# Maxima two tiles ahead, Fourier inputs ahead of the merge, and Fourier stages split by even and odd frequency

## The reference, cut to what matters

```python
def attend(q, k, v, lam):
    s = jnp.einsum('bhmqd,bhmkd->bhmqk', q, k, preferred_element_type=jnp.float32) * (B_QK ** -0.5)
    p = jax.nn.softmax(s, axis=-1)
    w = p[:, :, 0] - lam * p[:, :, 1]
    return jnp.einsum('bhqk,bhkv->bhqv', w.astype(v.dtype), v)

def fourier_mix(u):
    bsz, n, _ = u.shape
    uf = u.astype(jnp.float32).reshape(bsz, n, C_GROUPS, C_GROUP_DIM)
    y = jnp.fft.fft2(uf, axes=(1, 3), norm="ortho").real
    return y.reshape(bsz, n, C_WIDTH).astype(u.dtype)

def merge(y_a, y_b, y_c, mg, w_a_out, w_b_out, w_c_out, w_out):
    g_a, g_b, g_c = jnp.split(jax.nn.sigmoid(mg), N_BRANCH, axis=-1)
    y = g_a * (y_a @ w_a_out) + g_b * (y_b @ w_b_out) + g_c * (y_c @ w_c_out)
    return y @ w_out
```

## Time and profile before

| | us |
|---|---|
| median of 3 runs (2482.53 to 2489.82) | 2483.38 |
| profiled execution | 2483.57 |
| its span | 2481.80 |
| PE busy | 2329.3 (94%) |
| DVE busy | 1174.7 (47%) |
| ACT busy | 1126.4 (45%) |
| POOL busy | 726.2 (29%) |
| attention loop to the eighth z unit, layer 0 / 1 | 139.27 / 80.92 |
| from the end of cu to the first cz unit, layer 0 / 1 | 36.21 / 18.30 |

### The profile page before, as it was taken

One profiled execution on the slowest core, in us unless ns is written; L12 is line 12 of the kernel. 1 busy time (PEld: TensorE's weight loads), 2 busy tenths in 40 slices (PEclk: granted clock), 3 DMA queues, 4 the chain that ended last, 5 costly groups with the idle time before them and its releaser, 6 DMA issues.

```text
span 2481.8 us, 42435 instructions
## 1 busy us (share of the span) xinstructions
PE 2329.3 (94%) x15420; PEld 2027.9 (82%) x15420; DVE 1174.7 (47%) x2165; ACT 1126.4 (45%) x2329; POOL 726.2 (29%) x563
## 2 busy tenths in 40 slices
PE   6989999988999899999998889999989999988998
PEld 4758899858899798878886678988769989876998
DVE  3664334665335634441344663154473554436453
ACT  3454454454445534432455652222343554646443
POOL 2403554413455221122221012212222224211433
PEclk8989999989999999999999999999999999999999
DMA  7656965755865221122221012212223234221533
GB/s 286 237 183 198 313 199 186 251 195 189 289 233 199 92 83 60 56 72 98 80 78 51 26 52 97 82 52 93 87 75 102 94 106 158 70 84 52 170 136 136
DMA packets 159788, 328.73 MB, mean 132 GB/s; under 512 B 17696, under 2 KB 21024, under 8 KB 159520
## 3 DMA queue, kind: packets, MB, share of 16 engines
q1 hardware_dynamic: 159504, 325.80, 38.5%
q0 software_dynamic: 144, 0.98, 0.1%
HBM read 325.67 MB, written 1.05 MB: 132 GB/s over the span
## 4 chain that ended last, share of the span: by engine, by line
PE 77%; DVE 8%; issue 7%; ACT 4%; DMA 2%; POOL 1%; SPq 0%; POOLq 0%; ACTq 0%; DVEq 0%
PE PS L1690 15%; PE PS L1691 14%; PE PS L1692 14%; PE PS L1735 4%; PE PS L1737 4%; PE PS L1736 4%; PE PS L1671 2%; PE PS L1754 2%; PE PS L1753 2%; PE PS L1752 2%; DMA RAW<-stream 1%; PE PS L529 1%; ACT WORK L1014 1%; POOL WL L1607 1%; PE PS L1704 1%
## 5 line engine op out<-in xcount | busy, mean ns | idle before, releaser
L1607 POOL TENSOR_TENSOR WL<-RAW,WH 128x512 fp32r<-128x512 f32 x468 | 650.0, 1390 | 1680.6 <-ACT WH L1985 1680.1
L1690 PE MATMUL PS<-AR,WH 128*128 128x256 f32 (+1 forms) x2624 | 860.2, 328 | 15.0 <-DVE AR L1478 7.7
L1691 PE MATMUL PS<-AR,WH 128*128 128x256 f32 (+1 forms) x2624 | 841.6, 321 | 0.0
L1692 PE MATMUL PS<-AR,WL 128*128 128x256 f32 (+1 forms) x2624 | 841.5, 321 | 0.0
L1985 ACT ACTIVATE WH<-RAW 128x512 fp32r<-128x512 f32 x936 | 550.3, 626 | 438.9 <-DMA RAW<-stream 201.3
L2234 DVE TENSOR_TENSOR WL<-RAW,WH 128x512 fp32r<-128x512 f32 x468 | 395.9, 846 | 645.0 <-ACT WH L1985 643.3
L1690 PEld LDWEIGHTS PS<-AR,WH 128*128 128x128 f32 x2624 | 501.5, 191 | 97.9 <-issue 44.5
L1691 PEld LDWEIGHTS PS<-AR,WH 128*128 128x128 f32 x2624 | 501.8, 191 | 37.2 <-issue 2.4
L1692 PEld LDWEIGHTS PS<-AR,WL 128*128 128x128 f32 x2624 | 501.2, 191 | 36.7
L1735 PE MATMUL PS<-WH,AR 128*128 128x256 f32 x768 | 219.9, 286 | 0.0
L1736 PE MATMUL PS<-WL,AR 128*128 128x256 f32 x768 | 217.3, 283 | 0.0
(11 more groups left out here) (298 smaller groups left out, 3101.4 us busy)
## 6 DMA issues: line engine op xcount, KB each, us to landing
RAW<-stream SPq DMA_DIRECT2D x936, 256.0 KB, 2.9
WORK<-mods SPq DMA_DIRECT2D x144, 512.0 KB, 6.4
C<-consts SPq DMA_DIRECT2D x1, 1088.0 KB, 15.0
XX<-xT SPq DMA_DIRECT2D x1, 1024.0 KB, 10.2
XX<-ctxT SPq DMA_DIRECT2D x1, 1024.0 KB, 5.8
outT<-XX SPq DMA_DIRECT2D x1, 1024.0 KB, 4.8
C<-consts POOLq DMA_DIRECT2D x1, 960.0 KB, 7.5
WORK<-lam SPq DMA_DIRECT2D x1, 256.0 KB, 6.6
```

The costliest lines, as they stand in the source:

```text
L1607: pool.tensor_tensor(WL[:, u % 4, cut, :], RAW[:, (2 * u + 1) % 4, :, :], WH[:, u % 4, cut, :].bitcast(f32), ALU.subtract).then_inc(lo_don ...
L1690: pe.matmul(out, WH[:, u % 4, k, :], moving[:, 0, k, :], start=(k == 0), stop=False)
L1691: pe.matmul(out, WH[:, u % 4, k, :], moving[:, 1, k, :], start=False, stop=False)
L1692: last = pe.matmul(out, WL[:, u % 4, k, :], moving[:, 0, k, :], start=False, stop=(k == KC - 1))
```

## The change

1. `top(f+2)` follows `combine(f)` on DVE, with `top(0)` and `top(1)` ahead of the loop; `z_unit` and its weight low come one tile earlier. All eight bz units lie in the loop: a whole one ahead of it, the others from tile 1 + (x - 1) * last // 7, in three parts (9, 9 and 6 matmuls) in layer 0 and whole in layer 1.
2. The cu units stand ahead of bmerge. PE runs the four cu pairs right after the last value; heads 0 to 3 are turned after the second pair, 4 to 7 after the third. cu is no longer copied to V2: ACT copies half of each bank to FOLD and DVE writes the sum and the difference of the two token halves (`folded`). All of bmerge comes afterwards, as one loop.
3. Sums give the even frequencies, differences the odd ones, so stage one is four matmuls of 128 columns over one block for a pair of feature blocks y (an item) instead of eight. Columns of cu and cz and rows of the branch's output weights are laid out so that even and odd features of a group stand in two blocks; stage two works on them in the same way, with four matmuls an item. Items rotate over banks 4 to 7. ACT copies one half out (256 columns; in stage two the sines of both blocks) and DVE adds and subtracts; in stage two the results are interleaved, every other element. All of stage one comes ahead of stage two.

The diff, cut ("..."); of the old Fourier loops on PE, ACT and DVE only the first lines are repeated here.

```diff
-      ("bq", 8), ("bk", 8), ("bv", 8), ("bz", 8), ("bmerge", 16),
-      ("cu", 8), ("cz", 8), ("cmerge", 16), ("out", 8)]
+      ("bq", 8), ("bk", 8), ("bv", 8), ("bz", 8), ("cu", 8), ("bmerge", 16),
+      ("cz", 8), ("cmerge", 16), ("out", 8)]
...
+def unit_cuts(l):
+    return [(0, KC)] if l else [(0, 3), (3, 6), (6, KC)]
 def pieces(f, l):
-    per = per_head(l)
-    spread = [(p - 2) * (8 * per - 2) // (7 * per - 2) if p >= 2 else -1 for p in range(7 * per)]
-    return [p for p, at in enumerate(spread) if at == f]
+    parts, last = unit_cuts(l), 8 * per_head(l) - 1
+    if f < 0:
+        return [(0, p) for p in range(len(parts))]
+    begun = {1 + (x - 1) * last // 7: x for x in range(1, 8)}
+    return [(begun[f - p], p) for p in range(len(parts)) if f - p in begun]
 def ended(f, l):
-    per = per_head(l)
-    return [p // per for p in pieces(f, l) if p % per == per - 1]
+    return [x for x, p in pieces(f, l) if p == len(unit_cuts(l)) - 1]
+def fourier_items(l):
+    return [(p, y) for p in parts(l) for y in range(4)], 8 * l, 8 + 16 * l
...
-def turned_to(h, l):
-    b = stages(l)["bmerge"]
-    return (4, 6, 7, (b + 3) % 4, 5, (b + 2) % 4, 4, 6)[h]
+def turned_to(h):
+    return (4, 6, 7, 5)[h % 4]
...
-        def piece(g):
-            x, part = divmod(g, per)
-            u, ks = st["bz"] + x, KC // per
+        def piece(x, part):
+            u, (begin, end) = st["bz"] + x, unit_cuts(l)[part]
-            for k in range(part * ks, (part + 1) * ks):
+            for k in range(begin, end):
-            if part == per - 1:
+            if end == KC:
...
-            if h == 4:
+            if h == 3:
                 evicted(pe, st["bz"] + 7)
-            if h >= 6:
-                pe.wait_ge(gated, 24 * l + 8 + h - 5 + BEGUN)
+            if h >= 4:
...
+        for x, part in pieces(-1, l):
+            piece(x, part)
         for f in range(len(steps)):
             if f + 2 < len(steps):
                 score(f + 2)
             turn(f)
-            for p in pieces(f, l):
-                piece(p)
+            for x, part in pieces(f, l):
+                piece(x, part)
             if f:
                 value(f - 1)
         value(len(steps) - 1)
-        for g in range(7 * per, 8 * per):
-            piece(g)
-        for h in range(4):
-            head_turn(h)
+        for x in range(4):
+            token_pair(st["cu"], 0, 2 * x, H2, 2 * l, 4)
+            if x in (1, 2):
+                for h in range(4 * x - 4, 4 * x):
+                    head_turn(h)
         merge("bmerge", 1)
-        tokens("cu", 2 * l)
         for j in range(4):
-            pe.wait_ge(bank_read[(st["cz"] + j) % 4], earlier(st["cz"] + j))
...
+            pe.wait_ge(bank_read[(st["bmerge"] + j) % 4], earlier(st["bmerge"] + j))
+        dft = const("dft", 6 * P)
+        items, past, copied = fourier_items(l)
+        for i, (p, y) in enumerate(items):
+            if i >= 4:
+                pe.wait_ge(f1_read, past + i - 3)
+            for o in range(2):
+                x, bank = 2 * y + o, PS[:, 4 + i % 4, o * T:(o + 1) * T]
+                for e in range(2):
+                    last = pe.matmul(bank[:, e * P:(e + 1) * P], V2[:, 2 * p + e, x * P:(x + 1) * P],
+                                     dft[:, e * P:(e + 1) * P], start=True, stop=True)
+            last.then_inc(f1, 1)
+        for i, (p, y) in enumerate(items):
+            if i < 4:
+                pe.wait_ge(f1_read, past + len(items) - 4 + i + 1)
+            else:
+                pe.wait_ge(f2_read, past + i - 3)
+            for o in range(2):
+                x, bank = 2 * y + o, PS[:, 4 + i % 4, o * T:(o + 1) * T]
+                for e, (a, b) in enumerate(((0, P + 1), (P + 1, T))):
...
+        def halves(b):
+            def body(j):
+                done(b, 0, j)
+                bank = (b + j) % 4
+                if l == 0:
+                    act.activation(FOLD[:, j % 4, :], PS[:, bank, T:2 * T], ACT.Copy).then_inc(f_copied, 1)
+                elif j % 2:
+                    act.activation(FOLD[:, j % 4, :], PS[:, bank, 0:T], ACT.Copy).then_inc(bank_read[bank], 1)
+                next_high(b, 0, j)
...
+        exps(1)
         for x in ended(-1, l):
             z_unit(x)
             next_high(st["bz"], 0, x)
-        exps(1)
         for f in range(len(steps)):
             act.wait_ge(t2, tb + f + 1)
...
-        gate_functions()
-        z_unit(7)
-        next_high(st["bz"], 0, 7)
         sigmoids()
-        for k in range(KC):
-            act.wait_ge(gated, 24 * l + 8 + k + 1 + BEGUN)
-            act.activation(Y2[:, 0, k, t0:], YB[:, k, t0:], ACT.Copy).then_inc(yhi, 1)
+        take = halves(st["cu"])
+        for x in range(4):
+            take(2 * x)
+            take(2 * x + 1)
+            if x in (1, 2):
+                for k in range(4 * x - 4, 4 * x):
+                    act.wait_ge(gated, 24 * l + 8 + k + 1 + BEGUN)
+                    act.activation(Y2[:, 0, k, t0:], YB[:, k, t0:], ACT.Copy).then_inc(yhi, 1)
         merge("bmerge", 1)
-        looped(act, st["cu"], 8, 4, values(st["cu"], 2 * l))
...
+        items, past, copied = fourier_items(l)
+        for i in range(len(items)):
+            act.wait_ge(f1, past + i + 1)
+            act.activation(FOLD[:, i % 4, :], PS[:, 4 + i % 4, T:2 * T], ACT.Copy).then_inc(f_copied, 1)
+        for i in range(len(items)):
+            act.wait_ge(f2, past + i + 1)
+            if i >= 4:
+                act.wait_ge(f2_read, past + i - 3)
+            sines = PS[:, 4 + i % 4, :].rearrange("p (o t) -> p o t", o=2)[:, :, P + 1:T]
+            act.activation(SINES[:, i % 4, :, 1:P], sines, ACT.Copy).then_inc(f_copied, 1)
         z_gate("cz", 2)
...
+        def folded(j):
+            b = st["cu"]
+            if l == 0 or j % 2:
+                x = j if l == 0 else j - 1
+                row, cut = (j % 2 * 2 if l == 0 else 2), slice(j // 2 * 2 * P, (j // 2 + 1) * 2 * P)
+                if l:
+                    dve.wait_ge(bank_read[(b + j) % 4], earlier(b + j) + 1)
+                else:
+                    dve.wait_ge(f_copied, j + 1)
+                dve.tensor_tensor(V2[:, row, cut], PS[:, (b + x) % 4, 0:T], FOLD[:, j % 4, :], ALU.add)
+                ins = dve.tensor_tensor(V2[:, row + 1, cut], PS[:, (b + x) % 4, 0:T], FOLD[:, j % 4, :],
+                                        ALU.subtract)
+                ins.then_inc(bank_read[(b + x) % 4], 1)
+            next_low(b, 0, j)
...
         top(0)
+        top(1)
         for f in range(len(steps)):
-            if f:
-                combine(f)
-            for x in ended(f - 2, l):
+            combine(f)
+            if f + 2 < len(steps):
+                top(f + 2)
+            for x in ended(f - 1, l):
                 z_unit(x)
-            if f + 1 < len(steps):
-                top(f + 1)
-            if f == 0:
-                combine(0)
-            for x in ended(f - 2, l):
...
         refine(OC[:, 2, :, 2 * l:], OC[:, 3, :, 2 * l:])
-        for h in range(4):
+        for h in range(8):
             scale_head(h)
-        z_unit(7)
-        next_low(st["bz"], 0, 7)
-        for h in range(4, 8):
-            scale_head(h)
+            if h % 4 == 3:
+                folded(h // 2 - 1)
+                folded(h // 2)
         def b_low(k):
...
                               ALU.subtract).then_inc(y_done, 1)
         dve.wait_ge(bank_read[(st["bz"] + 7) % 4], earlier(st["bz"] + 7) + 1)
-        for k in range(KC):
-            dve.wait_ge(ot2, 8 * l + k + 1)
-            dve.scalar_tensor_tensor(YB[:, k, t0:], PS[:, turned_to(k, l), t0:], LM[:, 6 + l:7 + l],
-                                     SZ2[:, k, t0:], ALU.mult, ALU.mult).then_inc(gated, 1)
-            if k >= 2:
-                b_low(k - 2)
-        b_low(KC - 2)
-        b_low(KC - 1)
+        for x in range(2):
+            for k in range(4 * x, 4 * x + 4):
+                dve.wait_ge(ot2, 8 * l + k + 1)
+                dve.scalar_tensor_tensor(YB[:, k, t0:], PS[:, turned_to(k), t0:], LM[:, 6 + l:7 + l],
+                                         SZ2[:, k, t0:], ALU.mult, ALU.mult).then_inc(gated, 1)
+                if k >= 4 * x + 2:
+                    b_low(k - 2)
+            b_low(4 * x + 2)
+            b_low(4 * x + 3)
+            folded(4 + 2 * x)
+            folded(5 + 2 * x)
         merge("bmerge", 1)
-        lows("cu")
-        for p in parts(l):
...
-        dve.wait_ge(f2_read, 16 + 8 * l)
+        items, past, copied = fourier_items(l)
+        for i, (p, y) in enumerate(items):
+            dve.wait_ge(f_copied, copied + i + 1)
+            first, second = (x.rearrange("p (e c b) -> p c e b", e=2, c=2)
+                             for x in (PS[:, 4 + i % 4, 0:T], FOLD[:, i % 4, :]))
+            for o, op in enumerate((ALU.add, ALU.subtract)):
+                out = KB[:, 2 * y + o, p * T:(p + 1) * T].rearrange("p (c e b) -> p c e b", c=2, e=2)
+                ins = dve.tensor_tensor(out, first, second, op)
```

(16 more changed lines are left out.)

98 lines of the change are left out of this document (31 added, 67 removed).

## The result

The changed kernel takes 2446.11 us (median of 4 runs, 2436.42 to 2454.24) against 2486.58 of the kernel before (median of 4 in the same comparison): a ratio of 0.984, 95% interval 0.982 to 0.986. It is faster by 40 us. The forecast was 2428.7 with a range of 2412 to 2442: the sign was right, the gain of 54.9 us 14 too large, and the time 4 us outside the range. The profiled execution took 2447.45 us (span 2445.7).

What follows compares the result with a forecast made beforehand. TensorE bounds the kernel nearly everywhere, except the attention loops, bound by a circle of waits through DVE's maxima, exponentials and combine. Gains of 13.3, 3.4, 6.7, 20.7 and 10.8 sum to 54.9 us: 2483.6 to 2428.7 us, range 2412 to 2442.

Steps and rivals of the forecast that it cites:

- Part 1, layer 0: Layer 0's attention loop: maxima two tiles ahead break the circle of waits, 139.3 to 126 us, a gain of 13.3.
- The stalls: Layer 0's attention loop: TensorE waits for DVE at tiles where DVE is the later one, 16.9 us in all.
- Part 1, layer 1: Layer 1's attention loop: maxima two tiles ahead and whole z units, 80.9 to 77.5 us, a gain of 3.4.
- Part 2: cu ahead of the merge: waits of 2.7 us in layer 0 and 4.0 in layer 1 go, 6.7 us.
- The cover: cu and merge: TensorE's other work hides every later wait, tight in layer 1; otherwise 1 to 3 us return.
- Part 3: Fourier: half the matmuls and no copy wait, 15.5 and 7.5 us, gains of 20.7 and 10.8.
- disputed term: Fourier stage two on DVE, writes skipping every other element: 0.95 to 1.8 us an item, near end taken.
- A: Rival: the attention loops stay a chain of engines taking turns, +8.4 us, 2437; chance 0.14.
- B: Rival: TensorE sets nearly every loop step and half or more of the stalls goes, -15 us, 2414; chance 0.13.
- C: Rival: Fourier bound on DVE by doubled writes and slow first stage, +5 us, 2434; inside the forecast's 0.68.
- E: Rival: cover for cu and merge fails in layer 1, weights late, +3 to 6 us, 2434; inside the forecast's 0.68.
- D: Rival: waits keep TensorE's clock at its lower level throughout the loops, slower, up to 2560 us; chance 0.03.

Runs made afterwards that it cites:

- filled waits: Changed kernel with eight extra, unused matmuls ahead of each of five turns (tiles 1, 18, 22, 27, 31) in layer 0: 2432.11 us.
- Without GpSimd's overlap: Changed kernel with GpSimd's half of the weight low in layer 0 started one combine later: 2435.39 us.
- second trace: The changed kernel run and traced once more, with no edit: 2444.14 us, ratio 0.983.
- second better version: Changed kernel: z units begun per head, tile 2's score and weight low moved, last layer-0 unit in five parts, unit 0 scaled behind combine(1): 2418.48 us.
- score inside unit 0: Changed kernel with the score of tile 2 ahead of the last part of z unit 0 instead of behind the unit: 2440.40 us.
- units by head: Changed kernel with one number changed: layer 0's z units 1 to 7 begin at tiles 1, 5, 9, ... 25: 2429.79 us.
- finer units: Changed kernel with z units cut into quarters in layer 0 and halves in layer 1, over nearly all tiles: 2451.38 us.

## Why the prediction missed, point by point

The short form: part 1 in layer 0 failed, by 13.2 us. The sum put the clock at 1 us where it cost 9.2, and the holding of DVE's small steps by GpSimd, which lengthened the stalls by 2.9, at nothing.

**Base.** Of the 18.8 us between the forecast and the profiled 2447.45, 7.7 lie in stretches that the change leaves alone: 6.0 ahead of the first score, within the 14 us over which that point moves from trace to trace, 2.5 in the tail (the last 31 us at a clock of 0.89 against 0.94), -0.8 between. The profiled execution of before, 2483.57, also stood under the medians of its later runs, by 1 to 3 us (2484.3 to 2486.6). By medians the gain is 40 us where the trace shows 36 in all and 44 in the changed stretches. I took one trace as the base and gave it no scatter of its own.

**Part 1, layer 0 (13.3 forecast, 0.1 measured).** This is the step that failed. Its mechanism, PE or DVE the later one from tile to tile, holds: of the loop's 32 turns, every one that waits over half a us is one that the sum named (23, also named, waits for nothing, and 30 waits 0.45). Three terms were off, the clock's most of all:
- The clock, allowed 1 us, cost 9.2 in this trace (119.41 - 110.16; 9.3 by the filled waits) and 7.6 in the second one. That is 8.2 us more than allowed in the first. I read the old mean of 0.91 as a small thing, and in the kernel before it was one: there the chain through DVE and ACT set the time, and slow matmuls lay inside it. Its trace bears this out. Two of its steps, each from one combine of 512 keys (start of L1392) to the next, hold the same work on DVE, a z unit and maxima of 512 keys included (columns as in the earlier trace rows):

```profile
1426.55:1432.08 5.53, 4.03 (x12) 3.26 (x14) 4.33 (x7) 3.91 (x10) 1.27 (x1) 0.54 0.06 16
1443.97:1449.50 5.53, 1.98 (x16) 1.61 (x14) 4.33 (x7) 4.40 (x11) 1.27 (x1) 1.00 0.05 16
```

  With the clock at 0.54 in one and at 1.00 in the other, and PE busy 4.03 and 1.98 us of it, both take 5.53 us. Once PE's own work is on the path, the same 0.91 costs its full share.
- The stalls, 16.9 forecast, measured 19.8. For tiles 18, 22, 27 and 31 the sum had 2.6, 2.6, 1.9 and 1.9; they took 3.20, 3.20, 2.45 and 3.18. Without GpSimd's overlap they took 2.39, 2.39, 1.64 and 2.37 and all idle time 16.8. The missing 2.9 us is the shared port. With the waits that it lengthened went 6.2 us of the clock's cost too (PE's work fell from 119.41 to 113.22; against the second trace 4.6), though how much of that is one trace's luck stays open.
- PE's work at a clock of 0.99 was 110.2 where the sum has 126 - 16.9 - 1 = 108.1: 2.1 us. The steps of a head cost 3.64, 3.51, 3.74 and 3.93, 14.8 in all with 1.25 of waiting, so 13.6 of work, where I had 7.62 + 5.4 = 13.0 (the pieces of the 7.62 in fact add up to 7.54).

8.2 + 2.9 + 2.1 is the 13.2 that was missing. The port could be seen ahead of the prediction. POOL's weight lows are in the loop of before (10.95 us of its work in the earlier trace rows), and the small step of the maxima is held there at six tiles, for up to 0.86 us and each time to the end of one of them:

```profile
1429.07 0.86 DVE L1380 TENSOR_TENSOR BC<-BC,QN 128x2 f32<-128x2 f32 x1
1428.64 1.27 POOL L1607 TENSOR_TENSOR WL<-RAW,WH 128x512 fp32r<-128x512 f32 x1 [18.73 <-ACT WH L1985]
```

I counted no cost for running beside them.

**Part 1, layer 1 (3.4, measured 5.7).** Waits of 1.03 us at six tiles, 2.27 at turn(1) and 1.44 at turn(15), 9.9 in all where I had eight of 1.3, and PE's work 65.3 us where the sum has 67.1. The mean clock is 0.98, and ahead of turn(15) a step is stretched, at 2259.13.

**Part 2 (6.7, measured 5.7).** By layers it is 1.5 us where I had 2.7 and 4.2 where I had 4.0. The 2.7 were a wrong reading: in that stretch of the kernel before PE idled 16.72 - 15.55 = 1.2 us, none of it for scaled heads; the rest of the difference was PE's work being longer than my rates gave. The cover holds: PE is busy 137.49 of 137.49 us and 70.92 of 70.92, with no wait for a head, a fold or a weight. The second trace has 136.83 in layer 0; the 0.7 us between are slow matmuls behind the loop's last wait.

**Part 3 (20.7 and 10.8, measured 21.1 and 11.2).** Half the records at the old pace was right. The disputed term, writes that skip every other element, went to the near end. Groups by shape in layer 0's Fourier; L1500 writes runs, L1512 and L1515 every second element:

```profile
L1500 DVE TENSOR_TENSOR WORK<-PS,WORK 128x256 f32<-128x256 f32 x16 | 5.6, 412 | 0.3
L1512 DVE TENSOR_TENSOR WORK<-PS,WORK 128x256 f32<-128x256 f32 x8 | 3.4, 425 | 0.2 <-ACT WORK L1089 0.2
L1515 DVE TENSOR_TENSOR WORK<-PS,WORK 128x256 f32<-128x256 f32 x7 | 3.0, 426 | 0.0
```

425 ns against 412, 3% more. The Trainium skill's rule on SBUF lines (SBUF — State Buffer, section "Door 1: The DMA port swizzle"), by which fp32 may stride up to four elements for free, agrees within these 3%. The stall of 0.9 us at the entry was 0.6.

**The rivals.** A, the loops as a chain, was nearest by the time (2437), but its reason is wrong: with the units moved by one number the loops run well under it. B was wrong here; in the second better version PE is busy 95% of the layer 0 loop. C and E didn't occur. D had the mechanism and not its size: I priced the clock for the whole loop or at 1 us. Its share of 18% of the time at the lower level, which I computed for the kernel before, was already the right figure for the kernel after. The range missed by 4 us: nothing in it stood for a clock between those two, or for the scatter of the base. That A's time lies nearest is luck.

## What to carry to other kernels

When an edit moves the bound from a chain of other engines onto TensorE, take its clock from the rows of before and charge it in full; in the kernel before it was free because TensorE wasn't the bound. A place for filler work is worth as much as the filler: here the tile without it did best where TensorE has the most work of its own. And when small operations of DVE stand on the path, look at what GpSimd runs at that moment: one that is longer than elsewhere and ends with GpSimd's is held by it. Last, one trace is not a base: two of the same kernel differed by 1.6 us in this loop through the clock alone.

## What the runs showed of the hardware that was not expected

A DVE operation on one or two columns with two inputs in SBUF (0.16 or 0.22 us) took 0.42 to 1.08 us in these loops when it began during GpSimd's subtraction on 512 columns (1.26 us alone), and ended with it: 1337.19 + 0.66 = 1337.85 against 1336.57 + 1.26 = 1337.83; 1459.60 + 1.03 against 1459.28 + 1.33. The reciprocal, with one input, and reductions from PSUM took no longer beside it. GpSimd's own operation took 1.79 us when it began at 1402.56, during DVE's weight low (1402.54 to 1403.23).

Eight unused matmuls in a wait made the loop shorter: 648 matmuls in 130.6 us against 608 in 139.2. After single waits of 0.4 to 1.3 us the granted clock stayed up in layer 0's loops, with one exception: with the score inside unit 0 it fell between turns 13 and 14, which waited 1.25 and 0.92 us (the z matmuls start at 1382.41, 1382.84 and 1383.26, 0.43 apart), and behind the same two waits of the changed kernel it didn't. After waits of 1.8 to 3.2 us it sometimes fell and sometimes not. Behind 2.64 or 2.65 us at turn(1) the z matmuls went from 0.23 to 0.43 us apart in five traces, both of the changed kernel among them, and kept 0.23 with the units by head and with the finer units; behind 3.20 us at turn(18) the clock stayed up with the score inside unit 0 and fell in the five other traces that have this wait. What else decides it stays open.
